# Ten instead of four experts at fixed places, and the lists of the sorted ones made inside the expert loop

## The reference

```python
def moe(h, P, l):
    x = h.reshape(N, D)
    scores = sigmoid(x @ P["router_w"][l])
    biased = scores + P["router_bias"][l]
    ...   # the best 4 of 8 groups of experts
    _, eidx = lax.top_k(jnp.where(emask, biased, NEG), TOP_K)          # TOP_K = 6
    w = jnp.take_along_axis(scores, eidx, axis=-1)
    w = w / jnp.sum(w, axis=-1, keepdims=True) * ROUTED_SCALE
    gates = jnp.einsum("nk,nke->ne", w, one_hot(eidx, N_EXPERTS))
    hid = silu(einsum("nd,edf->nef", x, P["moe_w_gate"][l])) * einsum("nd,edf->nef", x, P["moe_w_up"][l])
    routed = jnp.einsum("nef,efd->nd", hid * gates[:, :, None], P["moe_w_down"][l])
    shared = (silu(x @ P["shared_w_gate"][l]) * (x @ P["shared_w_up"][l])) @ P["shared_w_down"][l]
    return (routed + shared).reshape(B, T, D)
```

## Time and profile before

| | us |
|---|---|
| median of three runs | 1652.82 (1651.82 to 1653.49) |
| the profiled execution | 1654.56 |
| its span in the profile | 1652.8 |
| expert loop on PE, first layer | about 365 to 829 |
| expert loop on PE, second layer | about 1181 to 1644 |

### The profile page before, as it was taken

The page is one execution under the profiler, slowest core; times in us unless marked ns, Lnnn a source line. Parts: engine busy times, 40 slices in busy tenths (PEclk is TensorE's granted clock), DMA queues, the critical chain, the costliest instruction groups (busy, mean ns, idle before and its releaser), DMA issues. The chain is left out here.

```text
span 1652.8 us, 25445 instructions
## 1 busy us (share of the span) xinstructions
PE 1534.0 (93%) x10085; PEld 914.1 (55%) x10087; DVE 380.8 (23%) x1081; ACT 285.8 (17%) x738; POOL 42.8 (3%) x84
## 2 busy tenths in 40 slices
PE   5999999999999888888989999999999988898887
PEld 3888788655444343334458878885545433343333
DVE  1215444341001000000132354443311100000002
ACT  1010242031111111111120103402211111111111
POOL 3001000000000000000020000000000000000000
PEclk8999999999999999999989999999999999999999
DMA  9995232469999999999999832235699999999995
GB/s 386 393 420 207 77 103 97 173 259 388 420 421 421 420 421 421 421 421 421 421 385 422 344 129 89 99 134 215 262 389 421 420 421 422 420 421 420 420 421 234
DMA packets 78281, 545.27 MB, mean 330 GB/s; under 512 B 9757, under 2 KB 9905, under 8 KB 13393
## 3 DMA queue, kind: packets, MB, share of 16 engines
q1 hardware_dynamic: 73440, 531.66, 78.9%
q0 software_dynamic: 4720, 11.97, 2.2%
HBM read 541.03 MB, written 2.56 MB: 329 GB/s over the span
## 5 line engine op out<-in xcount | busy, mean ns | idle before, releaser
L1058 PE MATMUL PS<-ring,region 128*32 128x512 f32 x2176 | 307.5, 644 | 67.3 <-DMA ring<-in_expert_blocks 52.9
L636 PE MATMUL PS<-region,ring 128*128 128x256 f32 x1088 | 244.9, 381 | 0.0
L1058 PEld LDWEIGHTS PS<-ring,region 128*32 128x32 f32 x2176 | 87.7, 117 | 253.1 <-issue 253.1
L636 PEld LDWEIGHTS PS<-region,ring 128*128 128x128 f32 x1088 | 203.8, 190 | 32.6 <-issue 5.3
L1017 PEld LDWEIGHTS PS<-region 128*128 128x128 f32 x1472 | 168.8, 193 | 38.4 <-issue 38.4
L1017 PE MATMUL PS<-region 128*128 128x128 f32 x1472 | 177.6, 279 | 0.0
L1837 DVE SCALAR_TENSOR_TENSOR region<-region,PS 128x256 f32<-128x256 f32 x44 | 18.5, 421 | 689.6 <-ACT region L1346 689.6
L1101 PE MATMUL PS<-region 128*128 128x512 f32 x352 | 158.8, 594 | 0.0
L1092 PE MATMUL PS<-ring,region 128*32 128x512 f32 x992 | 130.9, 595 | 1.2 <-ACT region L1350 1.2
L1058 PE MATMUL PS<-region 128*32 128x512 f32 x640 | 114.8, 607 | 10.6 <-DMA region<-in_expert_blocks 5.8
L1101 PEld LDWEIGHTS PS<-region 128*128 128x128 f32 x352 | 63.3, 190 | 66.7 <-issue 65.5
(11 more groups left out here) (280 smaller groups left out, 1142.2 us busy)
## 6 DMA issues: line engine op xcount, KB each, us to landing
ring<-in_expert_blocks SPq DMA_DIRECT2D x288, 1024.0 KB, 25.9
ring<-in_blocks SPq DMA_DIRECT2D x120, 1024.0 KB, 19.4
region<-in_expert_blocks SPq DMA_DIRECT2D x96, 1024.0 KB, 26.0
region<-post_rows POOLq DMA_DIRECT2D x8, 512.0 KB, 7.1
region<-in_shared_down SPq DMA_DIRECT2D x2, 1024.0 KB, 11.6
region<-in_mla_w_ukv POOLq DMA_DIRECT2D x2, 512.0 KB, 18.7
region<-in_post_pack POOLq DMA_DIRECT2D x2, 512.0 KB, 22.0
const<-in_consts POOLq DMA_DIRECT2D x1, 554.0 KB, 12.4
```

The source lines that it names most:

```text
L636: last = pe.matmul(PS[:, j % 2, m * T:(m + 1) * T], w[:, k, m * P:(m + 1) * P], hT[:, k, :], start=(k == 0), stop=(k == KC - 1))
L1058: last = pe.matmul(PS[i * SEG:(i + 1) * SEG, 0, :], xe[:, k, i * SEG:(i + 1) * SEG], w[:, k % 4, :], start=(k == 0), stop=(k == KC - 1), s ...
```

## The change

FIXED goes from 4 to 10: five groups of two experts, 18 groups of three, 23 in all. The matmuls for the token ranks, the gates and the lists go from before the loop into groups 1, 2 and 3 of it, into PSUM bank 1, with their copies on ACT and DVE. What is taken off the lists for a further pass is kept in `worked`. The gather of a group is cut in two halves with the hidden rows' transposes between them. The shared expert's down projection goes from groups 4 to 7 to groups 6 to 9. Of the 16 places, "hidden" (the transposed activations) gives way to "post", the rows for the norm after attention, free earlier; the rows for the norm after the experts get a stretch of their own (where "hidden" was) and are loaded when the shared expert's matmuls have read it.

```diff
-FIXED = 4
+FIXED = 10
-HOMES = (0, 1, 2, 3, 4, 5, 6, 7, 8, 9, "branch", "gates", "normed", "hidden", 10, 11)
+HOMES = (0, 1, 2, 3, 4, 5, 6, 7, 8, 9, "branch", "gates", "post", "normed", 10, 11)
...
-        postb = view(19456, 2, D)
+        postb = (view(19456, 2, D), view(17408, 2, D))
...
-                    elif at == "hidden":
-                        sp.wait_ge(shared_gu, (l + 1) * 2)
+                    elif at == "post":
+                        sp.wait_ge(x1_ready, (l + 1) * 4)
...
                 load_post(0)
-                pool.wait_ge(x1_ready, (l + 1) * 4)
+                pool.wait_ge(shared_gu, (l + 1) * 2)
                 apart(pool)
                 load_post(1)
...
-                gather(0, (4, 5), pe.snap(before_l * GROUPS) + (l + 1))
+                pe.wait_ge(hotT_ready, pe.snap(before_l * GROUPS) + (l + 1))
+                for half in range(2):
+                    gather(0, half, 4 + half)
                 sorted_order()
                 shared_gate_up(1, range(5, KC))
-                gates_across()
-                shared_transposes(0)
-                sorted_lists()
                 pe.wait_ge(zeros_ready, l + 1)
                 pe.wait_ge(ranks_read, l + 1)
-                clear_sums((6, 7))
+                release(clear_sums((6, 7)))
                 pe.wait_ge(xe_ready, pe.snap(before_l * (2 * GROUPS)) + (2 * l + 2))
                 clear_sums((4, 5))
+                shared_transposes(0)
                 shared_transposes(1)
-                pe.wait_ge(lists_ready, l + 1)
+                pe.wait_ge(order_ready, l + 1)
...
-                        gather(g + 1, (1, 3), done + (l + g + 2), halves_done + 2 * g if g else None)
+                        if g in (2, 3):
+                            pe.wait_ge(listT_ready, pe.snap(q * 2) + (g - 1))
+                        if g == 4:
+                            pe.wait_ge(lists_ready, q + 1)
+                        pe.wait_ge(hotT_ready, done + (l + g + 2))
+                        gather(g + 1, 0, 1)
                         transpose_hidden(g)
+                        if g:
+                            pe.wait_ge(og_ready, halves_done + 2 * g)
+                        gather(g + 1, 1, 3)
+                        if 1 <= g <= 3:
+                            pe.wait_ge(xe_ready, halves_done + (2 * l + 2 * g + 3))
+                            apart(pe)
+                            (token_ranks, gates_across, sorted_lists)[g - 1]()
                         if 0 < g < GROUPS - 1:
                             combine(g - 1)
-                        if 4 <= g < 8:
-                            shared_down(*divmod(g - 4, 2))
+                        if 6 <= g < 10:
+                            shared_down(*divmod(g - 6, 2))
...
                         take_hot(g)
+                        if g == 1:
+                            take_listT(ranksT_done, q, lambda v: v[:, P:3 * P])
+                        if g == 2:
+                            take_listT(gatesT_done, q, lambda v: v.rearrange("p (s t) -> p s t", s=4)[:, 0:4:3, :])
                         take_out(g)
...
                         hot_weights((g + 1) % GROUPS).then_inc(hotw_ready, 1)
-                        if g == 8:
+                        if g == 3:
+                            take_lists()
+                        if g == 10:
```

More of the change, by code:

```diff
@@ L87 @@
 UNITS = 18
[L90 to L91 removed]
+VECTOR_STEPS = (265, 260)
+PASS_STEPS = 5
 TAIL_STEPS = 13
@@ L357, in wide @@
             return ring[:, n % RING_SLOTS, :].rearrange("p (k n) -> p k n", k=4)
-        dead = {"gates": view(0, 2048), "normed": view(6144, 2048), "branch": view(10240, 2048), "hidden": view(17408, 2048)}
+        dead = {"gates": view(0, 2048), "normed": view(6144, 2048), "branch": view(10240, 2048), "post": view(19456, 2048)}
         def home(n):
@@ L982, in _ @@
                 last.then_inc(counts_done, 1)
[L983 to L994, removed]
                 def sorted_order():
@@ L1008, in gather @@
[L1008 to L1017, removed]
-                                                 start=(t == 0), stop=(t == 1), skip_group_check=True)
-                                if g and half == 0 and c == 0 and t == 0:
-                                    release(last, 2 if g - 1 < FIXED // 2 else 3)
-                        last.then_inc(xe_tr, 1)
+                def gather(g, half, bank):
+                    for c in range(4):
+                        for t in range(2):
+                            k = 4 * half + c
+                            last = pe.matmul(PS[:, bank, c * P:(c + 1) * P], h2x[:, t, k * P:(k + 1) * P], hotT[:, t, :],
+                                             start=(t == 0), stop=(t == 1), skip_group_check=True)
+                            if g and half == 0 and c == 0 and t == 0:
+                                release(last, 2 if g - 1 < FIXED // 2 else 3)
+                    last.then_inc(xe_tr, 1)
@@ L1023, in clear_sums @@
                 def clear_sums(banks):
                     for bank in banks:
-                        pe.matmul(PS[:, bank, :], zeros[:, 0:P], zeros[:, P:5 * P], start=True, stop=True, skip_group_check=True)
-                gather(0, (4, 5), pe.snap(before_l * GROUPS) + (l + 1))
+                        last = pe.matmul(PS[:, bank, :], zeros[:, 0:P], zeros[:, P:5 * P], start=True, stop=True, skip_group_check=True)
+                    return last
+                pe.wait_ge(hotT_ready, pe.snap(before_l * GROUPS) + (l + 1))
@@ L1113, in shared_down, with token_ranks, gates_across, sorted_lists @@
                             last.then_inc(shared_out, 1)
+                    def token_ranks():
+                        pe.matmul(PS[0:N_EXPERTS, 1, P:2 * P], sel[:, 0, :], ahead, start=True, stop=True, skip_group_check=True)
+                        pe.matmul(PS[0:N_EXPERTS, 1, 2 * P:3 * P], sel[:, 1, :], ahead, start=True, stop=False, skip_group_check=True)
+                        pe.matmul(PS[0:N_EXPERTS, 1, 2 * P:3 * P], sel[:, 0, :], ones, start=False, stop=True, skip_group_check=True).then_inc(ranksT_done, 1)
+                    def gates_across():
+                        pe.wait_ge(gw_ready, l + 1)
+                        for t in range(2):
+                            last = transpose(PS[0:N_EXPERTS, 1, 3 * t * P:(3 * t + 1) * P], gaten[:, t, :])
+                        last.then_inc(gatesT_done, 1)
+                    def sorted_lists():
+                        for i, seg in enumerate((1, 2, 0, 3)):
+                            last = pe.matmul(PS[:, 1, i * SORTED:(i + 1) * SORTED], listT[:, seg * P:(seg + 1) * P], place,
+                                             start=True, stop=True, skip_group_check=True)
+                        last.then_inc(lists_done, 1)
                     for g in range(GROUPS):
@@ L1473, in take_gains @@
                         dve.wait_ge(sum_done, l * SUMS + 2 * i + half + 1)
-                        step.add(ve.tensor_tensor(rows[:, t, cols], PS[:, 4 + 2 * t + half, :], postb[:, t, cols], ALU.mult))
+                        step.add(ve.tensor_tensor(rows[:, t, cols], PS[:, 4 + 2 * t + half, :], postb[rows_in - 1][:, t, cols], ALU.mult))
                 def add_rows(r, t, rows, done):
@@ L1862, in _ @@
                             dve.reg_mov(npass, dve.value_load(npass_i[0:1, 0:1], min_val=1, max_val=4))
[L1863 to L1867 removed]
+                    for segments, cap in ((slice(0, 2), CAP), (slice(2, SEGMENTS), LIGHT)):
+                        pstep(ve.tensor_scalar(worked[:, segments], worked[:, segments], float(cap), None, ALU.add))
                     assert pstep.n == PASS_STEPS, pstep.n
```

35 lines of the change are left out of this document (14 added, 21 removed).

## The result

The changed kernel takes 1668.46 us (median of 4 runs, 1666.72 to 1669.73) against 1653.15 (1651.82 to 1653.55): ratio 1.0093, 95% interval 1.0076 to 1.0111, slower by 15.3 us. The profiled execution took 1669.73 us, its span is 1667.9. I had forecast 1672.1, range 1664 to 1681.

What follows compares the result with a forecast made beforehand. PE sets the loop's pace while places are full, then DMA; the end is DMA's last dry moment plus blocks left. Per layer 8.8 + 2.3 + 0.45 - 2.15, second + 0.45: +19.3 on 1652.82 gives 1672.1 us, range 1664 to 1681.

Steps and rivals of the forecast that it cites:

- Groups of two at the start: Loop start: three more groups of two at PE's pace let DMA rest, +8.8 us a layer.
- early blocks: Blocks 12 to 15, issued before the loop: 10.1 us of transfers earlier, counted at nothing; rival: lasting gain, -8 us a layer, 0.06.
- DMA last runs dry in group 5: Sign in the loop: DMA share under one in groups 1 to 4, full behind group 5's first matmul.
- PE first waits for a block in group 12: Sign in the loop: PE waits for blocks first around group 12; before group 10 would prove the forecast wrong.
- PE stopped at 1329.87: Old kernel's second-layer loop: the chain jumps there from PE to a transfer, and is DMA again and again afterwards.
- Work within the loop: Groups 1 to 3: ranks, gates' transposes and lists count in full, +2.3 us a layer, bounds 1.5 and 4.
- The gather's halves: Group 0 and the last group: down waits for the later second half, +0.45 us each; the first layer's last is swallowed.
- Before the loop: Ranks, gates' transposes and lists gone ahead of the loop: -2.15 us a layer, bounds 0 and -3.5.
- the block's time: Loop's transfers: 2.52 us per block, from 410.5 us over 163 blocks of the old kernel's second layer.
- my sum: Whole kernel: +9.4 us in the first layer and +9.85 in the second, together +19.3 us.

Runs made afterwards that it cites:

- late_pairs: Kernel before with ten fixed experts, but only two groups of two at the start and three as groups 12 to 14: 1652.40 us, ratio 1.0002.
- order_wait: Changed kernel in which SP waits for the order again before block 12: 1668.45 us, ratio 1.0107 to before.
- padded: Kernel before with an unused tensor of 64 bytes a partition ahead of `region`, which then begins at byte 132352: 1645.31 us, ratio 0.9964.
- worked_last: Changed kernel with `worked` behind `region` instead of ahead, so `region` begins at byte 132320: 1674.32 us, ratio 1.0131 to before.
- places_only: Kernel before with only the change's new set of places, second stretch for the norm's rows and their waits: 1654.20 us, ratio 1.0016.

## Why the prediction was right, and where it was off

Direction and mechanism were right, and the time lay in the range, 3.6 us below the forecast.

- **Groups of two at the start** (+8.8 a layer). Right: late_pairs shows that only their place costs, order_wait that early blocks don't pay, the stretches that DMA last runs dry in group 5, and PE first waits for a block in group 12, as I had said. Twice I failed to carry the same rule to `shared_down` in the expectations, where it gave 1.7 and 3.4 us more a layer. I had read the chain as if PE stopped at 1329.87; there it only released a place, and first waited at 1333.76, in the same group. And of the four early blocks only three came early, which cost nothing, as early blocks count for nothing.
- **Work within the loop** (+2.3). Groups 1 to 3 are 1.0, 0.2 and 1.2 us longer: 2.4.
- **The gather's halves** (+0.45 each in group 0 and at the end). 15.8 against 15.3 us, and a tail longer by 0.4.
- **Before the loop** (-2.15). -2.3 us in the second layer, -0.7 in the first. The changed kernel had 3.4 us at the lower clock in both layers, the one before in the second alone. Like with like it is -2.3: 78.9 or 80.5 with the old order, 76.6 or 78.3 with the new one, without and with such a piece.
- **The term that was mis-sized is the block's time.** I took 2.52 us from before and held it fixed. The loop grew by 10.4 and 10.3 us, not by 8.8 + 2.3 + 0.45 = 11.6, as the stream went from 421 to 423 GB/s. The cause lay in a line that I had passed over, `worked = sb(...)`.
- **The schedule by itself cost somewhat more than my sum.** At nearly like rates the loops grow by 12.2 to 13.0 us (changed against padded, worked_last against before). With a block's time of 2.51 us, for 423 GB/s, and the measured 2.4, the terms give 9.1 + 2.4 + 0.45 = 12.0; the rest, 0.2 to 1.0 us a layer, stays open. For the whole kernel worked_last gives 1.0131 x 1653 - 1653 = 21.7 us (interval 19.0 to 24.1), and the padded one 1.0093 / 0.9964 = 1.0129, 21 us. My sum was 19.3, inside that interval at its lower end.

So the schedule was put about 2 us too low (which the interval doesn't quite tell from nothing), and 5 to 6 us that have nothing to do with the schedule came off. That the two partly cancel, and the forecast missed by 3.6 us only, is luck.

What stays open: the 2.6 us of places_only, which lie in stages that scatter too much in single profiles, and what decides in which executions the clock falls there.

## What to carry to other kernels

Where a loop goes from compute's pace to the transfers' pace, its end is set by the last moment at which the transfers ran dry; look for it, count the work left behind it, and put the groups that need fewer bytes per compute time behind it, where they cost nothing, not ahead. A prefetch that starts earlier gives nothing if the queue runs dry later anyway. A step of the chain from an engine to a transfer is not yet a wait: look in the timeline for where the engine stands idle. Before a difference of 1 or 2 us is called scatter, compare the granted clock of the two stretches. When a change adds a tensor ahead of a large one that transfers write into, look at where the large one now starts.

## What the runs showed of the hardware

Blocks of 1 MB, 8192 bytes a partition, of which a quarter went to `region` and the rest to the ring (which begins at byte 16512 in all kernels): with `region` at 132352 or 132608 the loop's stream ran at 423 GB/s; at 132288 at 421; at 132320 at 420. From landing to landing a block took 2.43 or 2.44 us in the first case if it went to `region`, and 2.48 or 2.49 in all others, the ring's blocks included. 132352 and 132608 are multiples of 256, the other three starts are not; 16512 is a multiple of 128, so that 128 is not enough. A multiple of 512 (132608) gave nothing over 132352. For the whole kernel it was 5 to 6 us in 1650 by the ratios, 4 to 5 of them in the loops. A ring at a multiple of 256, and why the writes care, were not tried.

TensorE's granted clock fell to 0.50 for 3.4 us in some executions and not in others, at the same place of the same program: 1.6 us each where PE sets the pace.
